# Layer 0's gate and up products by seven quarter products, and three attention output blocks by token halves

## The reference

```python
mod_x = (sc @ ada_w[l] + ada_b[l])[:, None, :]
sh1x, sc1x, g1x, sh2x, sc2x, g2x = jnp.split(mod_x, 6, axis=-1)
hx = modulate(rms_norm(x, norm1_g[l]), sh1x, sc1x)
ox, oc = even_mixer(hx, hc, ...)        # layer 0; odd_mixer in layer 1, latent tokens only
x = x + g1x * ox
x = x + g2x * swiglu(modulate(rms_norm(x, norm2_g[l]), sh2x, sc2x), ffn_w1[l], ffn_w3[l], ffn_w2[l])
# layer 0: the same for the context tokens xc

def swiglu(h, w1, w3, w2):
    return (jax.nn.silu(h @ w1) * (h @ w3)) @ w2
```

## Time and profile before

| what | value |
|---|---|
| median of three executions | 1565.41 us |
| profiled execution, its own time | 1566.63 us |
| its span, first to last instruction | 1564.8 us |
| TensorE busy in the span | 1522.8 us (97%) |
| VectorE | 884.1 us (56%) |
| ScalarE | 618.3 us (40%) |
| GpSimd | 572.9 us (37%) |
| granted clock of TensorE, mean | 0.995 |

### The profile page before, as it was taken

One profiled execution on the slowest core, in us unless ns is written; L12 is line 12 of the kernel. 1 busy time (PEld: TensorE's weight loads), 2 busy tenths in 40 slices (PEclk: granted clock), 3 DMA queues, 4 the chain that ended last, 5 costly groups with the idle time before them and its releaser, 6 DMA issues.

```text
span 1564.8 us, 25514 instructions
## 1 busy us (share of the span) xinstructions
PE 1522.8 (97%) x10533; PEld 1258.7 (80%) x10533; DVE 884.1 (56%) x1398; ACT 618.3 (40%) x944; POOL 572.9 (37%) x316
## 2 busy tenths in 40 slices
PE   6999999899999999999999999999999999999997
PEld 3888864478888888888888888865568899989896
DVE  5898777668456634333333233666724863636454
ACT  5744235563422211221122234335454553636354
POOL 0030036413233232332222223346554564646562
PEclk9999999999999999999999999999999999999999
DMA  9532110052333333333333221210003232322322
GB/s 376 219 119 70 45 38 1 3 197 100 108 111 131 131 112 135 118 124 135 137 133 128 74 78 58 82 41 1 1 28 105 79 131 91 113 91 95 121 83 80
DMA packets 46914, 157.51 MB, mean 101 GB/s; under 512 B 5040, under 2 KB 9520, under 8 KB 45264
## 3 DMA queue, kind: packets, MB, share of 16 engines
q1 hardware_dynamic: 46368, 155.69, 28.5%
q0 software_dynamic: 432, 0.20, 0.1%
HBM read 153.90 MB, written 2.10 MB: 100 GB/s over the span
## 4 chain that ended last, share of the span: by engine, by line
PE 84%; DVE 5%; issue 2%; ACT 1%; POOL 1%; DMA 0%; DVEq 0%; POOLq 0%
PE psum L2365 51%; PE psum L2890 12%; PE psum L2916 7%; PE psum L2613 3%; PE psum L2581 2%; PE psum L2512 1%; PE psum L2410 1%; DVE mx L1654 1%; PE psum L2587 1%; DVE osb L1758 1%; PE psum L2585 1%; PE psum L2583 1%; PE psum L2629 1%; PE psum L2441 1%; POOL acc L845 1%
## 5 line engine op out<-in xcount | busy, mean ns | idle before, releaser
L2365 PE MATMUL psum<-act,whi 128*128 128x512 f32 (+2 forms) x2560 | 556.5, 337 | 0.0
L902 POOL TENSOR_TENSOR wlo<-raw,whi 128x1024 fp32r<-128x1024 f32 (+1 forms) x100 | 242.8, 2429 | 600.7 <-ACT whi L938 600.7
L2365 PEld LDWEIGHTS psum<-act,whi 128*128 128x128 f32 x2560 | 394.5, 189 | 55.4 <-issue 1.8
L2365 PE MATMUL psum<-act,wlo 128*128 128x512 f32 (+2 forms) x1280 | 331.0, 335 | 0.0
L2365 PEld LDWEIGHTS psum<-act,wlo 128*128 128x128 f32 x1280 | 200.1, 189 | 26.8
L938 ACT ACTIVATE whi<-raw 128x1024 fp32r<-128x1024 f32 (+1 forms) x118 | 123.0, 1043 | 206.5 <-DMA raw<-weights_dram 206.1
L1501 DVE SCALAR_TENSOR_TENSOR product<-adr,cb 128x1024 f32<-128x1024 f32 x128 | 177.6, 1419 | 6.4 <-DMA adr<-adat_dram 3.4
L1549 DVE SCALAR_TENSOR_TENSOR tmps<-psum,rs 128x512 f32<-128x512 f32 (+1 forms) x100 | 49.4, 536 | 183.9 <-PE psum L2365 183.8
L2890 PE MATMUL psum<-fhi,fwhi 128*128 128x256 f32 x532 | 149.9, 282 | 0.8 <-ACT xT L1320 0.6
L2890 PE MATMUL psum<-flo,fwhi 128*128 128x256 f32 x532 | 149.5, 281 | 0.0
L1997 DVE SCALAR_TENSOR_TENSOR xT<-psum,mod,xT 128x512 f32<-128x512 f32 x72 | 42.5, 628 | 141.9 <-PE psum L2365 141.9
(11 more groups left out here) (271 smaller groups left out, 2522.9 us busy)
## 6 DMA issues: line engine op xcount, KB each, us to landing
raw<-weights_dram SPq DMA_DIRECT2D x118, 512.0 KB, 3.8
adr<-adat_dram SPq DMA_DIRECT2D x80, 512.0 KB, 4.9
fraw<-weights_dram SPq DMA_DIRECT2D x38, 512.0 KB, 3.5
ada_w<-ada_dram SPq DMA_DIRECT2D x8, 1024.0 KB, 14.0
fraw<-weights_dram SPq DMA_DIRECT2D x24, 320.0 KB, 2.8
xT<-x_in_dram SPq DMA_DIRECT2D x3, 1024.0 KB, 16.9
xT<-x_in_dram SPq DMA_DIRECT2D x2, 1536.0 KB, 7.9
cb<-crow_dram SPq DMA_DIRECT2D x2, 1024.0 KB, 9.8
```

Of the source, the lines that this page charges most:

```text
L902: nc.gpsimd.tensor_tensor(wlo[:, s, 0:w], raw[:, s, 0:w], whi[:, s, 0:w].bitcast(F32), ALU.subtract).then_inc(sem("s_lo"), 1)
L2365: last = MM(out_[:, o:o + t1 - t0], w_, a_[:, t0:t1], start=k == order[0] and j == 0, stop=k == order[-1] and j == 2)
```

## The change

**Layer 0's FFN** no longer belongs to the stream. Both layers have the same code: three plain tiles, and 19 units, which in layer 0 work on token halves of 384 columns. The areas in SBUF are laid out anew; the high parts of weight quarters lie in 8 places in turn in layer 0 and 10 in layer 1, where before layer 1 had two sets of 7. The copies of the products 1, 7, 6 and 5 (`staged`) have one buffer each, where before they had two. The groups are 3, 4, 4, 4, 3, 4 tiles in layer 0 and 3, 4, 4, 3, 4, 4 in layer 1 (3, 5, 5, 4, 5 before).

**The tokens of an FFN** are now finished before the first product: `token_scaled` (VectorE, x times root), `token_input` (ScalarE, scale and shift in place, then the high part), `token_rest` (VectorE, the low part), for 2 halves x 8 channel tiles. The first plain tile takes them half by half (`first_plain_tile`).

**The last three attention output blocks** of both layers are made by token halves in the order `END` (`end_of_output`), with mean and root for each half.

**The late adaLN tiles** have the ring of three up to tile 24 only. Tiles 25 to 27 stand between the half blocks of the attention output; the others in the plain tiles, the units and the `w2` pairs (`late_in_pairs`). Up to tile 47 they have one buffer, `adr_late[0]`, and a load is issued when all products before it are done; from tile 48 on two.

```diff
-GROUPS = [[(0, 8), (8, 7), (15, 7)], [(0, 3), (3, 5), (8, 5), (13, 4), (17, 5)]]
+GROUPS = [[(0, 3), (3, 4), (7, 4), (11, 4), (15, 3), (18, 4)], [(0, 3), (3, 4), (7, 4), (11, 3), (14, 4), (18, 4)]]
...
-LATE_OUT = [1, 2, 1, 2, 1, 1]
+LATE_OUT = [1, 2, 2, 2, 2]
+LATE_RING = N_LATE0 + sum(LATE_OUT)
+LATE_END = 3
+N_LATE_FFN = len(LATE) - LATE_RING - LATE_END
+N_BOTH = 48
...
+def is_split(n):
+
+    return BLOCKS[n]["kind"] == "out" and BLOCKS[n]["m"] >= SPLIT
...
+def late_in_pairs():
+
+    out, i = [], len(LATE) - N_LATE_FFN
+    for p in PAIRS[0]:
+        if p["kind"] == "plain":
+            n = [1, 2, 1][p["t"]]
+        elif p["kind"] == "unit":
+            n = 2 if i < N_BOTH else 3
+        else:
+            n = int(p["m"] in (2, 4))
+        n = min(n, len(LATE) - i)
+        out.append(range(i, i + n))
+        i += n
+    return out
...
             def load_late(i):
-                if i >= AT_RING:
-                    sp.wait_ge(sem("s_atd"), late_sums(i - AT_RING + 1))
-                sp.dma_start(adr[:, i % AT_RING, :], adat[i, :, :]).then_inc(sem(f"s_at{i % AT_RING}"), 16)
+                if i < LATE_RING:
+                    if i >= AT_RING:
+                        sp.wait_ge(sem("s_atd"), late_sums(i - AT_RING + 1))
+                    place = adr[i % AT_RING]
+                elif i < N_BOTH:
+                    sp.wait_ge(sem("s_atd"), late_sums(i))
+                    place = adr_late[0]
+                else:
+                    sp.wait_ge(sem("s_atd"), late_sums(max(N_BOTH, i - 1)))
+                    place = adr_late[i % 2]
+                sp.dma_start(place[:, :], adat[i, :, :]).then_inc(sem(f"s_at{i % AT_RING}"), 16)
...
+            def token_input(L, h, k):
+
+                act.wait_ge(*token_z(L, h, k))
+                if (h, k) == (0, 0):
+                    act.wait_ge(sem("s_modA"), 3 + 2 * L)
+                    act.wait_ge(sem("s_mod"), 7 + 2 * L)
+                row = bf[L][h][:, k, :]
+                for a, e, c in token_parts(L, h):
+                    r_ = row[:, a - HALF[L] * h:e - HALF[L] * h]
+                    last = A(r_, r_, ACT.Identity, scale=modA[:, 2 * L + 1, k, c:c + 1], bias=mod[:, L, 24 + k, c:c + 1])
+                last.then_inc(sem("f_h"), 1)
+                act.wait_ge(*token_h(L, h, k))
+                A(form_high(L, token_form(h, k), k % KH), row, ACT.Copy).then_inc(sem("f_h"), 1)
...
+            def plain_gate(L, t, h):
+
+                act.wait_ge(*(half_done(L, h) if t == 0 else plain_done(L, t, 0)))
+                if t >= 1:
+                    act.wait_ge(*plain_gated(L, t - 1))
+                A(staged[L][0][:, h, :], bank(plain_banks(t)[0] + h)[:, 0:HALF[L]], ACT.Silu).then_inc(sem("f_y"), 1)
...
+                    elif i < N_BOTH:
+                        w, product = adr_late[0][:, :], products[1][:, :]
+                        dve.wait_ge(sem("s_atd"), t)
+                    else:
+                        w = product = adr_late[i % 2][:, :]
...
+            def end_of_output(L):
+
+                if L == 0:
+                    late_bias(0, 24, 32, N_SHIFT2)
+                end_residual(L, 0, 0)
+                add_square(NORM_BY[("out", L)], SPLIT - 1, TOKENS[L])
+                end_residual(L, 0, 1)
+                end_add(L, 0, 0)
+                if L == 0:
+                    late_modulation(LATE_RING)
+                end_residual(L, 1, 0)
+                end_add(L, 1, 0)
+                if L == 0:
+                    late_modulation(LATE_RING + 1)
+                end_residual(L, 0, 2)
+                end_add(L, 0, 1)
+                if L == 0:
+                    late_modulation(LATE_RING + 2)
+                end_residual(L, 1, 1)
+                token_scaled(L, 0, 0)
+                token_scaled(L, 0, 1)
+                token_rest(L, 0, 0)
+                token_scaled(L, 0, 2)
+                token_rest(L, 0, 1)
+                end_add(L, 1, 1)
+                token_scaled(L, 0, 3)
+                token_rest(L, 0, 2)
+                token_scaled(L, 0, 4)
...
+                    late_in_pair(L, j, False)
+                    sum_low(L, j + 1, "S2")
                     if p["kind"] == "unit":
-                        quarter11(p["n"])
-                    sum_low(j + 1, "S2")
+                        quarter11(L, p["n"])
+                    late_in_pair(L, j, True)
+                    sum_low(L, j + 1, "S1")
                     if p["kind"] == "unit":
-                        quarter22(p["n"])
-                        quarter21(p["n"])
...
+            def first_plain_tile(L):
+
+                for h in range(2):
+                    for k in range(KT):
+                        if (h, k) == (0, 4):
+                            end_mean(L, 1, 0)
+                            end_mean(L, 1, 1)
+                        pe.wait_ge(*token_high(L, h, k))
+                        pe.wait_ge(*token_low(L, h, k))
+                        x = token_form(h, k)
+                        fh_, fl_ = form_high(L, x, k % KH), form_low(L, x, k % KH)
+                        for w in range(2):
+                            wh_, wl_ = plain_piece(L, 0, w, k)
+                            for i, (w_, a_) in enumerate(((wh_, fh_), (wh_, fl_), (wl_, fh_))):
+                                last = MM(plain_out(L, 0, w, h), w_, a_, start=k == 0 and i == 0, stop=k == KT - 1 and i == 2)
+                    last.then_inc(sem("f_blk"), 1)
+
...
+            def product(L, j, n, x):
 
                 wx, fx = PRODUCT[x]
                 before = {6: 1, 5: 6, 3: 5, 4: 7}
+                g = PAIRS[L][j]["g"]
                 if x in before:
-                    pe.wait_ge(*copied(n, before[x]))
+                    pe.wait_ge(*copied(L, n, before[x]))
                 if x == 1 and n >= 2:
-                    pe.wait_ge(*hidden_low_done(n - 2))
-                if x == 1 and n - 1 in LAST_UNIT:
-                    pe.wait_ge(sem("f_res"), KT * LAST_UNIT.index(n - 1) + 6)
-                if x == 1 and n - 2 in LAST_UNIT:
-                    pe.wait_ge(sem("f_res"), KT * LAST_UNIT.index(n - 2) + 8)
-                if x == 2 and n == 0:
-                    pe.wait_ge(*ev(N1 - 2))
-                    pe.wait_ge(*ev(N1 - 1))
+                    pe.wait_ge(*tile_low(L, PLAIN + n - 2))
+                if x == 1 and n - 1 == LAST_UNIT[L][g - 1]:
+                    pe.wait_ge(*w2_added(L, KT * (g - 1) + 6 - L))
+                if x == 1 and n - 2 in LAST_UNIT[L]:
+                    pe.wait_ge(*w2_added(L, KT * LAST_UNIT[L].index(n - 2) + 7))
                 if x == 2 and n >= 1:
-                    pe.wait_ge(*quarter(n - 1, "c11"))
-                pe.wait_ge(*piece_high_done(j, wx))
-                pe.wait_ge(*piece_low_done(j, wx))
-                wh_, wl_ = high_piece(j, wx), low_piece(j, wx)
+                    pe.wait_ge(*quarter(L, n - 1, "c11"))
+                pe.wait_ge(*piece_high_done(L, j, wx))
+                pe.wait_ge(*piece_low_done(L, j, wx))
+                wh_, wl_ = high_piece(L, j, wx), low_piece(L, j, wx)
                 for k in range(KH):
-                    if n == 0 and x == 1:
-                        pe.wait_ge(sem("f_fhi"), k + 1)
-                        pe.wait_ge(sem("f_loD"), k + 1)
-                    fh_, fl_ = fhi[:, k, FORM[fx], :], flo[:, k, FORM[fx], :]
+                    if n == 0 and fx in T_FORM:
+                        pe.wait_ge(*form_high_done(L, k))
```

1434 lines of the change are left out of this document (859 added, 575 removed).

## The result

| | us |
|---|---|
| before, median of 4 executions | 1565.01 (1564.19 to 1565.69) |
| after, median of 4 | 1555.48 (1554.32 to 1557.09) |
| ratio | 0.994, 95% interval 0.9923 to 0.9957 |
| profiled execution after, span | 1554.2, mean clock 0.992 |

It is faster, as forecast, but by 9.5 us where 24.9 were forecast, and 1555.48 lies above the upper end of the stated range, 1554.

A forecast was written before the change was run, and what follows sets the result against it. TensorE, busy throughout layer 0's FFN, was taken as the bound. Terms -42.9 + 9 + 2.5 + 4 + 1 + 0.5 + 0 + 1 = -24.9 gave 1540.5 us; own range 1534 to 1547, 8 in 10 within 1528 to 1554.

The forecast's parts named there:

- Layer 1: Layer 1: shorter plain blocks offset junction losses, net 0 (-3 to +4); one w2 group more, +1 us (0 to 3).
- The units of layer 0: Layer 0's 19 units: VectorE's late tiles delay TensorE in the first six units, +4 us (0 to 10).
- the third plain tile: First group's w2 blocks: TensorE waits for the third plain tile's low part in VectorE's queue, +2.5 us (0 to 6).
- the junction: Layer 0's attention output to FFN: late tiles delay the first token, then ScalarE sets the pace, +9 us (4 to 14).
- The products: Layer 0's FFN: matmuls of 384 columns at 175 ns, gain -42.9 us (-41 to -44).
- VectorE's round: Layer 0's first six units: late loads, products and other work take VectorE 15.2 to 16 us against TensorE's 14.7.
- one more group: Layer 1: one w2 group more, and a closing block of 1.4 instead of 1.8 us, +1 us (0 to 3).
- A new wait for weights (high parts): Sign of being wrong: TensorE waits in the units for high parts or GpSimd's lows, which the sum has at nothing.
- Seam: Layer 0 to layer 1: 4.2 us blocks cover 3.4 us of eviction, low part and squares, +0.5 us (0 to 3).
- The w2 blocks: Layer 0's FFN: w2 keeps its 528 matmul pairs at 352.7 ns, 186.2 us.
- the 1 us for waits at the groups' starts: Layer 0's w2 blocks: a wait at each group's start is possible, +1 us (0 to 3).
- the one in which every late product waits for GpSimd: Rival, layer 0: each late product loses up to 1.3 us; six units of 18 us; -12 in all, 1553 us; chance 0.18.

The follow-up runs named there:

- e2: Changed kernel with a place of its own for late tile 26, so its load overlaps use of tile 25: 1552.84 us, ratio 0.9928 to the kernel before.
- e11: Changed kernel scaling each second-half piece in one ScalarE operation, leaving out the context's own scale and shift: 1551.12 us, one execution.
- e5: Changed kernel with 56 extra matmuls of 128 columns in TensorE's wait for the third tile's low part: 1555.18 us, ratio 0.994 to the kernel before.
- e12: Changed kernel with 34 extra matmuls of 256 columns in TensorE's wait for the third tile's low part: 1551.31 us, one execution.
- e1: Changed kernel with late tile 31 and the gate bias moved behind the third plain tile in VectorE's queue: 1551.08 us, ratio 0.9919 to the kernel before.
- e3: Changed kernel with layer 0's FFN late tiles spread into the w2 blocks, fewer in each unit: 1550.39 us, ratio 0.9916 to the kernel before.
- e4: Changed kernel with S3 and S2 high parts behind copies of products 7 and 6 in layer 1's first units: 1550.16 us, ratio 0.9913 to before.
- e6: Changed kernel with GpSimd's low part of layer 1's second projection block held back at layer 0's end: 1552.4 us, ratio 0.9924 to the kernel before.
- e7: Changed kernel with late products from tile 25 on cut to 32 of 1024 columns, loads kept: 1534.51 us, ratio 0.981 to the kernel before.
- e10: Changed kernel with 30 extra matmuls of 128 columns in TensorE's wait for the third tile's low part: 1556.27 us, one execution.

## Why the prediction was wrong

The main gain and the places of loss were forecast; what failed is four terms of the sum. Layer 1 stood at +1 and was +6.8: the sum had nothing for a new wait inside its units. The units of layer 0 stood at +4 and were +9, the third plain tile at +2.5 and was +6.6, the junction at +9 and was +11.1.

- **The products, right.** 174.5 ns against 175; a weight load for every 384 columns did no harm.
- **Junction, +9 forecast, +11.1.** Mechanism and start (5.7 for 6 us) as forecast. The term was sized short by 2: a piece of the second half is 1.44 us, not 1.3 (its two scalings with the step to the copy take longer than I had from 0.38 + 0.495), and one of the first half 1.2, not 1.1. e2 gives 2.0 of it back from the side of the loads, e11 shows ScalarE's part.
- **Third plain tile, +2.5 forecast, +6.6** (31.82 over the 25.2 of 24 x 1.05). The walk through VectorE's queue was right in its order and 1.6 us short. What failed besides is that a wait was counted at its own length: 4.1 us of idle TensorE bring 1.5 to 1.8 us at the lower clock (e5, e12). The other 0.7 or so is not clock: e12 too is 0.5 us over 60 pairs at 349.7 ns behind its wait. The term ended just outside its bounds (0 and 6). One late tile's place decides most of it (e1).
- **Units, +4 forecast, +9** over 19 x 14.67: 5.9 and 3.2 us in the two groups with two late tiles a unit. The step that failed is the size of VectorE's round, 15.2 to 16 us in the forecast. Once it paces TensorE it takes 16.9 (513.31 to 530.17): late products 6.5 us where I had 5.7 to 6.4, the load's wait 3.1 for 2.8, other work 7.2 for 6.7. The slack was about as forecast: VectorE fell back by 2.3 us against TensorE in the first unit, which lost only 0.3, and then no further. One late tile a unit costs nothing (e3), and from tile 48 on none was lost, as forecast. Which part of the round to shorten, the load's wait by a second buffer or the two products that meet GpSimd, no run has tried.
- **Layer 1, 0 and +1 forecast, +6.8.** The step that failed is that both terms hold nothing for waits inside the units: they price the blocks, the junction and one more group, and take the units as they were before. A new wait for weights (high parts) "in the units, which my sum has at nothing" stands among the signs of being wrong; what came is a wait for a copy that stands behind such a high part. I did not see that the change puts S3's high part ahead of the copy of product 7 in ScalarE's queue. It cost 5.1 us in five groups (e4). This is the largest miss against the value taken, though just inside the two terms' upper bounds added (4 and 3). The rest lies between the first output block and the first unit, 103.4 us for 101.56 where net 0 was forecast; no run takes it apart.
- **Seam, +0.5 forecast, +2.0**, and the clock at 0.59 and 0.56 for 4 us behind it, another 1.6 us that no term held (not so in all kernels, below). I had VectorE's work as 3.4 us of 4.2; two of its operations met GpSimd's and took 3 us each, and parting one of them gave the 2.0 back (e6).
- **The w2 blocks**, 3 ns a pair cheaper, gave 1.6 us back, and the 1 us for waits at the groups' starts was not needed.

Of the rivals, the one in which every late product waits for GpSimd has a time (1553) close to the measured one, and its mechanism is there at a part of its size. It had 18 us a unit and every late product 1.3 us longer. In the first group they took 1.59 on the mean and waited 13.2 us for their loads; in the round shown, the two that ran beside GpSimd's work took 1.91 and 2.19 us and the other two 1.26 and 1.23, so 1.6 of its 16.9 us. No run parts them there; e7 shows that the loads without the products' time cost nothing, and e3 that one tile a unit fits. That the time is close is luck: 5.1 us of it are layer 1's swap, which that case did not have.

## What to carry to other kernels

When a change regroups work, read each engine's queue at the start of every group: an item that waits for a slow engine must not stand ahead of a copy that TensorE waits for (5.1 us here, by one swap). Side work goes where the engine that does it has its idle time (VectorE in a group's w2 blocks, 13 of 33 us), not by count of steps, and no more per step than load + products + adds fit in it. A TensorE wait of microseconds (1.9 and more here) is to be priced with the slower matmuls that can follow it: some 1.6 us here, and nothing where another engine sets the pace anyway.

## What was not expected of the hardware

- The same wait did not always bring the lower clock. Behind the 4 us wait for the third tile it fell in all six kernels that had it. Behind the wait of 2.6 to 2.8 us at the start of the first plain tile it fell in the changed kernel, e5, e10, e11 and e12 and not in e1, e3, e4 and e6, with the same instructions; behind the 1.9 us before the mean it fell in the changed kernel, e2, e3, e5 and e10 and not in e1, e4, e7, e11 and e12. Where it fell, it was back after some 3 to 4 us, or about 7 behind the third tile's wait in the changed kernel and e11. The price differs by place: nothing in the first plain tile, 1.6 us behind the mean. So a profile with such a wait has a luck of up to 1.6 us in it.
- In e2 the two late products that no longer wait for a load took 2.19 and 2.18 us where they had taken 1.23: GpSimd's operations of 389.03 and 394.08 us lie beside them. Moving a wait away can move work onto the other engine's operations: the edit gave 2.0 of the 3 us expected. That this overlap is the whole of the difference isn't shown.
- A pair of matmuls in w2 took 349.7 ns where the pairs of the old FFN had 352.7 on the mean; the old ones have 258 columns in place of 256 in the gate and up products. Whether that is the reason isn't shown.
